# Norms, sums and output product chunk by chunk in a two-layer hybrid block

## The chip, the cores and the metric

One core of a Trainium2 chip runs the whole program. The metric is device time in microseconds (us), the median of several runs. All arithmetic is in f32. TensorE is PE here, VectorE DVE, ScalarE ACT, GpSimd POOL, and SP is the engine that issues most DMAs.

## The reference, cut to what matters

Two layers process 256 context tokens and 256 latent tokens, 1024 features each. `mod` is a projection of a conditioning vector and gives shift, scale and gate for each half of a layer.

```
a   = rmsnorm(h, norm_mix) * (1 + scale) + shift
u   = a @ w_in                                  # 1024 -> some 3900 columns
y   = three groups of scans (SSD, HGRN2, gated DeltaNet), each with its own grouped RMS norm
h  += gate * (y @ w_out)
f   = rmsnorm(h, norm_ffn) * (1 + scale) + shift
h  += gate * (routed(f) + shared(f))            # 64 experts, top 8 by sigmoid score, and one shared
out = rmsnorm(h, norm_final)                    # latent tokens, after layer 1
def rmsnorm(x, w): return x * rsqrt(mean(x * x) + 1e-6) * w
```

In layer 1 only the latent tokens are carried past the scans.

## The kernel before, in words

The 512 tokens are four chunks of 128 rows: 0 and 1 are context, 2 and 3 latent. `h` holds them with tokens on the partitions. `LIVE` names the chunks that go past the scans: four in layer 0, two (2 and 3) in layer 1. Each engine runs its own program in a fixed order, written out by hand; they meet in semaphores, through helpers named `wait`. There is no planner: what stands first in an engine's list runs first, and what follows waits behind it. Most instructions go through one-line helpers, so the profile shows the helpers' lines: L1098 (`tt`), L1101 (`ts`), L1104 (`stt`) and L1107 (`cp`) on DVE, L832 on ACT, L1732 (matmul) and L1736 (transpose by the identity) on PE.

**A norm.** `sumsq` (L1155) on DVE sums the squares of each live chunk, all chunks in a row, into `st`. `rstd` on ACT makes the inverse root as exp(-0.5 ln(...)). `norm_turn` on DVE scales each chunk of `h` into one of two row buffers `X[:, c % 2]`; PE transposes it into two PSUM banks; the first four of eight feature blocks go to `featT` through DVE (`turned`, L1174), the other four through ACT (L858), with scale and shift applied on the way.

**The head.** PE multiplies the conditioning vector by eight blocks of `w_mod` as their DMAs arrive, `mod_turn` and `mod_add` put the result where the norm needs it, and the norm of all chunks follows. The projection's small product (wsm) is the first reader of `featT`.

**The output product.** `w_out` comes in four blocks of 256 columns through a ring of two slots. For each block PE multiplies all live chunks, gives the slot back (`ring_used`), and DVE adds gate times product to `h`. After the fourth block the second norm runs, and the router's product (rw) is its first reader. SP's list from here on: a block of w_out whenever a slot is given back, then sh_gate and sh_up of the shared expert through the same ring, each when its slot is given back, a wait until DVE has added the last block (`wo_sb`), twelve loads of 1 MB that fill four expert slots, then for each live chunk the store of its FFN rows to DRAM (`f_dram`, in the profile ffn_rows) as ACT has written them to `X[:, c % 2]`, the routing weights' store, and sh_down. The loops over the two X buffers mean that ACT's third row copy waits for the store of the first (`x_stored0`), the fourth for that of the second. PE waits for all row copies (`ftok_sb`) before it computes the experts' positions (matmuls of `mask` with `triS`, past_ in the profile, and ones).

**The experts.** 64 steps in a pipeline of four slots. POOL gathers rows of ffn_rows, PE multiplies, and POOL scatters with addition into two sums in DRAM, even experts to ffn_sum_even (`acc_dram`), which also holds the shared expert's result, odd ones to ffn_sum_odd (`acc_odd`). A further branch serves experts with over 128 rows; it adds to the even sum.

**Between the layers and at the end.** When both sums are complete and POOL has passed its branch, SP loads the odd sum into the memory of featT (`yraw` and `featT` are the same bytes) and the even one into `sums`. DVE waits for both, does three passes over each chunk (even plus odd, times gate, plus h), then signals `h_ready`. Then the next layer's first norm runs, or the final norm with two passes a chunk (scale, then weight) and the store of the output. The next layer's parameters are copied from PSUM between the square sums and the scaling.

## Time and profile before

| | us |
|---|---|
| median of 3 runs (2814.79 to 2819.05) | 2814.97 |
| the profiled execution: its time | 2812.39 |
| its span in the trace | 2810.7 |
| PE busy (87% of the span) | 2448.0 |
| DVE busy (45%) | 1266.5 |
| ACT busy (23%) | 643.9 |
| POOL busy (22%) | 610.6 |

Times in the trace count from the span's start. A busy share is an average over stages: the scans run to about 650 us in layer 0 and from about 1750 to 2080 in layer 1, the experts from 838 to 1515 and from 2178 to 2775. In the timeline a row gives start, busy time, engine, line, operation, output and inputs, the count of merged instructions and, in brackets, how long the engine had been idle and what released it. A granted clock of 1.00 is 2.4 GHz on TensorE, 0.50 is 1.2 GHz. DMA landing times run from issue to the semaphore.

### The profile page before, as it was taken

The numbers are of one execution on the slowest core, as the hardware profiler recorded it, in microseconds if no ns is written. First come the engines' busy times: TensorE is split into PE (matmuls) and PEld (weight loads), VectorE is DVE, ScalarE is ACT, GpSimd is POOL, SyncE is SP. The second block draws the span as 40 slices with busy tenths as digits, with TensorE's granted clock in tenths as the row PEclk, the third lists the DMA queues.
The fourth block names the chain that finished last, engine by engine and source line by source line (L and its number), as shares of the span: only waits on it lengthen the run. The fifth ranks groups of instructions, "written<-read, shape, count | busy, mean of one in ns | idle before, by whom it ended". The sixth has DMA issues, their size and how long they took to land.

```text
span 2810.7 us, 45706 instructions
## 1 busy us (share of the span) xinstructions
PE 2448.0 (87%) x15116; PEld 1632.2 (58%) x15117; DVE 1266.5 (45%) x2832; ACT 643.9 (23%) x1146; POOL 610.6 (22%) x640
## 2 busy tenths in 40 slices
PE   5999888886789999999996798888877999999994
PEld 2347788885645555555553345787865555555552
DVE  4433487875333333333332553467853333333333
ACT  2116343231111111111110114523321111111111
POOL 0000354550002222222221000245320122222221
PEclk9999899997899999999998799999989999999998
DMA  6643100001539999999996251200017899999993
GB/s 259 244 175 76 19 2 1 1 1 35 195 136 319 367 352 349 344 343 341 364 336 192 99 201 60 49 1 1 1 43 276 314 365 374 376 354 361 364 367 115
DMA packets 187920, 574.26 MB, mean 204 GB/s; under 512 B 55742, under 2 KB 99078, under 8 KB 148870
## 3 DMA queue, kind: packets, MB, share of 16 engines
q1 hardware_dynamic: 162950, 520.48, 49.8%
q0 software_dynamic: 24832, 51.97, 8.0%
q8 instruction: 82, 1.34, 0.2%
q14 instruction: 56, 0.46, 0.0%
HBM read 554.89 MB, written 53.15 MB: 216 GB/s over the span
## 4 chain that ended last, share of the span: by engine, by line
PE 58%; DVE 15%; DMA 14%; issue 5%; ACT 4%; POOLq 2%; DVEq 2%; ACTq 1%; POOL 0%; SPq 0%
PE ps L1732 53%; DMA featT<-ffn_rows,idx_in 8%; PE ps L1736 5%; DVE R L1098 3%; DMA R<-ffn_rows,idx_in 3%; ACT R L832 2%; DVE featT L1098 2%; DVE ring L1098 1%; POOLq L744 1%; DVE R L1372 1%; DMA R<-in_exp_up 1%; ACT L832 1%; DVEq L1095 1%; DVE R L1101 1%; DMA R<-ffn_sum_even 1%
## 5 line engine op out<-in xcount | busy, mean ns | idle before, releaser
L1732 PE MATMUL ps<-R 128*64 128x256 f32 (+6 forms) x9040 | 1391.4, 379 | 68.9 <-DVEq L1377 19.3
L1732 PEld LDWEIGHTS ps<-R 128*64 128x64 f32 (+2 forms) x9040 | 850.1, 162 | 477.2 <-issue 250.5
L832 ACT ACTIVATE R<-ps 128x256 f32<-128x256 f32 (+3 forms) x395 | 175.5, 444 | 1047.7 <-PE ps L1732 993.7
L1098 DVE TENSOR_TENSOR R<-R,ps 128x256 f32<-128x256 f32 (+2 forms) x250 | 143.7, 575 | 439.8 <-ACT R L832 368.5
L1732 PE MATMUL ps<-featT,ring 128*128 128x512 f32 (+1 forms) x768 | 312.5, 563 | 0.3 <-issue 0.3
L1732 PE MATMUL ps<-ring,R 128*128 128x128 f32 (+2 forms) x1200 | 242.4, 334 | 16.3 <-DVE ring L1098 7.8
L1732 PEld LDWEIGHTS ps<-featT,ring 128*128 128x128 f32 x768 | 147.2, 196 | 161.8 <-issue 156.9
L1732 PEld LDWEIGHTS ps<-ring,R 128*128 128x128 f32 x1200 | 191.9, 196 | 49.1 <-issue 28.7
L1101 DVE TENSOR_SCALAR R<-ps,idx_out 128x512 f32<-128x512 f32 x128 | 96.1, 751 | 270.9 <-PE ps L1732 270.9
L1107 DVE COPY R<-ps 128x512 f32<-128x512 f32 (+2 forms) x280 | 153.8, 549 | 129.9 <-PE ps L1736 96.4
L669 POOL TENSOR_TENSOR R<-ring,lev 128x512 f32<-128x512 f32 x56 | 73.0, 1303 | 618.5 <-DVEq L1334 307.3
L768 POOL DMA_INDIRECT ffn_sum_even<-R,idx_out x64 | 94.5, 1476 | 481.2 <-DVE idx_in L1098 354.6
L768 POOL DMA_INDIRECT ffn_sum_odd<-R,idx_out x64 | 98.1, 1532 | 436.9 <-issue 291.7
L1736 PE MATMUL ps<-ident,featT 128*128 128x128 f32 x864 | 124.2, 290 | 67.4 <-DMA featT<-ffn_rows,idx_in 32.3
L832 ACT ACTIVATE R<-ps,idx_out 128x512 f32<-128x512 f32 x128 | 88.2, 689 | 382.8 <-PE ps L1732 382.8
L1736 PEld LDWEIGHTS ps<-ident,featT 128*128 128x128 f32 x864 | 98.4, 147 | 110.3 <-DMA featT<-ffn_rows,idx_in 49.8
L737 POOL DMA_INDIRECT featT<-ffn_rows,idx_in x96 | 95.1, 991 | 242.4 <-issue 242.4
L1036 ACT ACTIVATE R<-ps 128x512 f32<-128x512 f32 x128 | 76.5, 598 | 193.7 <-PE ps L1736 187.2
L1736 PE MATMUL ps<-ident,R 128*128 128x128 f32 x616 | 103.6, 285 | 15.2 <-DMA R<-ffn_rows,idx_in 12.8
L1732 PE MATMUL ps<-ring,featT 128*128 128x256 f32 x512 | 115.1, 386 | 1.0 <-issue 1.0
L1732 PEld LDWEIGHTS ps<-ring,featT 128*128 128x128 f32 x512 | 98.7, 194 | 17.5 <-issue 4.0
L669 POOL TENSOR_TENSOR R<-R,lev 128x512 f32<-128x512 f32 x56 | 72.9, 1301 | 119.2 <-PE ps L1732 85.9
(201 smaller groups left out, 1974.3 us busy)
## 6 DMA issues: line engine op xcount, KB each, us to landing
R<-in_exp_gate SPq DMA_DIRECT2D x128, 1024.0 KB
R<-in_exp_up SPq DMA_DIRECT2D x128, 1024.0 KB
R<-in_exp_down SPq DMA_DIRECT2D x128, 1024.0 KB
R<-in_w_mod SPq DMA_DIRECT2D x48, 1024.0 KB, 7.4
ring<-in_w_in SPq DMA_DIRECT2D x30, 1024.0 KB, 5.3
ring<-in_w_out SPq DMA_DIRECT2D x8, 1024.0 KB, 8.0
ffn_sum_odd<-zero SPq DMA_DIRECT2D x6, 512.0 KB, 11.1
ffn_rows<-X SPq DMA_DIRECT2D x6, 512.0 KB, 5.4
```

Of the source, the lines that this page charges most:

```text
L669: do(G.tensor_tensor(NTm[:, run % 2, :, :], AT[u % 2][:, :, :], lev[:, UNITS[u][1], j, :].unsqueeze(1).to_broadcast([P, HH, P]), ALU.mult) ...
L737: pool.indirect_dma_start(xg[s][0:n, :], None, f_dram, bass.IndirectOffsetOnAxis(idxG[s][0:n, 0:1].bitcast(U32), 0), bounds_check=TOK - 1, ...
L744: wide = pool.value_load(more[0:1, at_], min_val=0, max_val=1)
L768: pool.indirect_dma_start((acc_dram, acc_odd)[s % 2], bass.IndirectOffsetOnAxis(idxS[s][0:n, 0:1].bitcast(U32), 0), oe[s % 2][0:n, :], Non ...
L832: do(C.activation(out_, in_, func, **kw), name)
L1036: do(C.activation(xgT[b][:, 0:4, :].rearrange("p k t -> p (k t)"), ps[:, 0, :], ACT.Identity), "xt_sb")
L1095: dve.drain()
L1098: do(V.tensor_tensor(out_, a, b, op), name)
L1101: do(V.tensor_scalar(out_, a, s1, s2, op0, *(() if op1 is None else (op1,))), name)
L1107: do(V.tensor_copy(out_, in_), name)
L1732: return MM(out_, lhsT, rhs, start=start, stop=stop)
L1736: return nc.tensor.transpose(out_, in_, ident[0:k, 0:k])
```

## The change

Five things are done.

1. **Norms by chunk, root on ACT.** Each chunk's square sum has its own semaphore step; ACT takes `Sqrt` of the mean, DVE the reciprocal, and scales at once. The mixer's grouped norm also uses Sqrt and a reciprocal. ACT writes all eight feature blocks of a chunk, except chunk 3, which is still split. The second norm's transposes go to banks 0 to 3.
2. **Head.** Parameters are transposed and copied first; chunks 0 and 1 are scaled and transposed before PE's eighth w_mod block.
3. **Output product.** Blocks 0 and 1 as before. Blocks 2 and 3 are taken together, chunk by chunk: PE waits for both blocks, multiplies one chunk by both, and DVE adds and norms it; the transposes of a chunk stand behind the next chunk's product. Both ring slots are given back after the last chunk. SP's own list is unchanged here but for the count that it waits for.
4. **Sums.** They lie in `R` and no longer in featT. The even sum is loaded as soon as the even scatters are complete, the odd one behind POOL's branch as before, each in two halves. DVE adds, gates, adds to h and norms one chunk after the other. The branch for large experts now adds to the odd sum.
5. **Tail.** The final norm is done by chunk, scale and weight in one pass; its weight is loaded before the last experts end.

Removed lines of functions that are shown above are left out below; indentation is cut by eight.

```diff
@@ -298,7 +298,9 @@
...
-sums = R[:, ex:ex + NT * DM].rearrange("p (c f) -> p c f", c=NT)
+sums, sums2 = (R[:, a:a + NT * DM].rearrange("p (c f) -> p c f", c=NT) for a in (4 * BW * 8, 9 * BW * 8))
+fin = ring[:, 1, :, :].rearrange("p k n -> p (k n)")[:, 0:DM]
@@ -392,6 +394,14 @@
...
+def xt_bank(q, c):
+    return bank((4, 0)[q] + 2 * (c % 2), 2)
+def by_dve(c):
+    return KT // 2 if c == NT - 1 else 0
@@ -518,7 +528,7 @@
...
-        wait("wo_sb", N_OUT, l)
+        wait("wo_sb", 2 + nl, l)
@@ -572,8 +582,16 @@
...
+        else:
+            sp.dma_start(fin, A["norm_final"].rearrange("(o f) -> o f", o=1).to_broadcast([P, DM])).then_inc(S["head_loaded"], 16)
...
+        halves = ((live[:nl // 2], "sums_loaded"), (live[nl // 2:], "sums_b"))
+        wait("scattered0", 8 * NE, l)
+        for cs, name in halves:
+            rows = slice(cs[0], cs[-1] + 1)
+            sp.dma_start(sums[:, rows, :], acc_dram.rearrange("(c p) f -> p c f", p=P)[:, rows]).then_inc(S[name], 16)
@@ -595,13 +613,10 @@
...
-        for b in range(2):
-            wait(f"scattered{b}", 8 * NE, l)
-        rows = slice(live[0], NT)
-        sp.dma_start(yraw[:, rows, :], acc_odd.rearrange("(c p) f -> p c f", p=P)[:, rows]).then_inc(S["sums_loaded"], 16)
-        sp.dma_start(sums[:, rows, :], acc_dram.rearrange("(c p) f -> p c f", p=P)[:, rows]).then_inc(S["sums_loaded"], 16)
-    sp.wait_ge(S["h_ready"], DEPTH + 1)
-    sp.dma_start(grow[:, 0, :], A["norm_final"].rearrange("(o f) -> o f", o=1).to_broadcast([P, DM])).then_inc(S["head_loaded"], 16)
+        wait("scattered1", 8 * NE, l)
+        for cs, name in halves:
+            rows = slice(cs[0], cs[-1] + 1)
+            sp.dma_start(sums2[:, rows, :], acc_odd.rearrange("(c p) f -> p c f", p=P)[:, rows]).then_inc(S[name], 16)
@@ -842,27 +857,34 @@
...
+    def root(at_, l, c):
+        wait("sumsq", at_, l)
+        f(st[:, 4 + c:5 + c], st[:, c:c + 1], ACT.Sqrt, "rstd", scale=1.0 / DM, bias=cst[:, 0:1])
+    def feats(q, n, c, l):
+        if n == 0:
+            act.wait_ge(S["mod_sb"], (1, 4, 3, 6)[2 * q + l])
+        wait("xT_ps", q * NT + n + 1, l)
+        for k in range(by_dve(c), KT):
+            ins = C.activation(featT[:, k, tk(c)], xt_bank(q, c)[:, tk(k)], ACT.Identity,
+                               scale=amul[:, q, k, c // 2:c // 2 + 1], bias=mod[:, 24 * q + k, c // 2:c // 2 + 1])
+        do(ins, "feat_a")
...
+        live_ = LIVE[l] if q else range(NT)
+        at_ = q * (NT + 1) + 1
+        for n in range(2):
+            root(at_ + n, l, live_[n])
+        if q == 0 and l == 0:
+            mod_row(0)
+        for n, c in enumerate(live_):
+            feats(q, n, c, l)
+            if n + 2 < len(live_):
+                root(at_ + n + 2, l, live_[n + 2])
@@ -1006,11 +1028,10 @@
...
-        wait("sumsq", 2, l)
+        wait("sumsq", NT + 1, l)
...
-        f(ssq[:, cs, 0:2], ssq[:, cs, 0:2], ACT.Ln, scale=1.0 / HW, bias=cst[:, 0:1])
-        f(ssq[:, cs, 2:10], ssq[:, cs, 2:10], ACT.Ln, scale=1.0 / HD, bias=cst[:, 0:1])
-        f(ssq[:, cs, :], ssq[:, cs, :], ACT.Exp, "rstd", scale=-0.5)
+        f(ssq[:, cs, 0:2], ssq[:, cs, 0:2], ACT.Sqrt, scale=1.0 / HW, bias=cst[:, 0:1])
+        f(ssq[:, cs, 2:10], ssq[:, cs, 2:10], ACT.Sqrt, "rstd", scale=1.0 / HD, bias=cst[:, 0:1])
@@ -1150,28 +1170,34 @@
...
+    def sumsq(c):
+        V.tensor_tensor_reduce(out=X[:, c % 2, :], in0=h[:, c, :], in1=h[:, c, :], scale=1.0, scalar=0.0,
+                               op0=ALU.mult, op1=ALU.add, accum_out=st[:, c:c + 1])
...
+    def inv_rms(at_, l, c):
+        wait("rstd", at_, l)
+        do(V.reciprocal(st[:, 8 + c:9 + c], st[:, 4 + c:5 + c]))
+    def norm_rows(q, l, n, c):
+        if n >= 2:
+            wait("xT_ps", q * NT + n - 1, l)
+        sumsq(c)
+        inv_rms(q * (NT + 1) + n + 1, l, c)
+        ts(X[:, c % 2, :], h[:, c, :], st[:, 8 + c:9 + c], None, ALU.mult, name="xn")
+    def head(l):
+        wait("prm_ps", 1, l)
+        cp(prm[:, :], ps[:, 7, 0:N_PRM], "prm_sb")
+        cp(lowv[:, 0, :], low[:, l:l + 1, :].rearrange("p o t -> p (o t)"))
+        ts(lowv[:, 2, :], lowv[:, 0, :], -1.0, 1.0, ALU.mult, ALU.add)
+        ts(lowv[:, 1, :], lowv[:, 0, :], 1e-30, float(2.0 ** 40), ALU.max, ALU.mult, "low_c")
...
+        for k in range(by_dve(c)):
+            ins = V.tensor_scalar(featT[:, k, tk(c)], xt_bank(q, c)[:, tk(k)],
@@ -1180,15 +1206,14 @@
...
-        sumsq(range(NT))
-        wait("prm_ps", 1, l)
-        cp(prm[:, :], ps[:, 7, 0:N_PRM], "prm_sb")
-        cp(lowv[:, 0, :], low[:, L1, :].rearrange("p o t -> p (o t)"))
-        ts(lowv[:, 2, :], lowv[:, 0, :], -1.0, 1.0, ALU.mult, ALU.add)
-        ts(lowv[:, 1, :], lowv[:, 0, :], 1e-30, float(2.0 ** 40), ALU.max, ALU.mult, "low_c")
...
+            head(0)
+            for c in range(2):
+                norm_rows(0, 0, c, c)
...
-        norm_turn(0, l)
+            for c in range(2, NT):
+                norm_rows(0, 0, c, c)
+            turned(0, NT - 1, NT - 1, 0)
@@ -1543,16 +1570,20 @@
...
-        for n in range(N_OUT):
+        for n in range(2):
...
-            b0 = 4 + 2 * (n % 2)
...
-                o = X[:, 0, 0:2 * BW].rearrange("p (c f) -> p c f", c=2)
-                tt(o, ps[:, b0 + j, :].rearrange("p (c f) -> p c f", c=2), grow[:, j, cols].unsqueeze(1).to_broadcast([P, 2, BW]), ALU.mult)
+                o = sqo[:, 0, 0:2 * BW].rearrange("p (c f) -> p c f", c=2)
+                tt(o, ps[:, 4 + 2 * n + j, :].rearrange("p (c f) -> p c f", c=2), grow[:, j, cols].unsqueeze(1).to_broadcast([P, 2, BW]), ALU.mult)
...
-        sumsq(live)
-        norm_turn(1, l)
+        for n, c in enumerate(live):
+            wait("wo_ps", 2 + n + 1, l)
+            tt(sqo[:, 0, 0:2 * BW], ps[:, 4 + c, :], grow[:, c // 2, 2 * BW:DM], ALU.mult)
+            tt(h[:, c, 2 * BW:DM], h[:, c, 2 * BW:DM], sqo[:, 0, 0:2 * BW], ALU.add, "wo_sb")
+            norm_rows(1, l, n, c)
+        turned(1, len(live) - 1, live[-1], l)
@@ -1700,24 +1731,29 @@
...
+        if l + 1 < DEPTH:
+            head(l + 1)
...
-        wait("sums_loaded", 16 + 32, l)
-        for c in live:
-            tt(sums[:, c, :], sums[:, c, :], yraw[:, c, :], ALU.add)
+        for n, c in enumerate(live):
+            if n == 0:
+                wait("sums_loaded", 16 + 32, l)
+            if n == len(live) // 2:
+                wait("sums_b", 32, l)
+            tt(sums[:, c, :], sums[:, c, :], sums2[:, c, :], ALU.add)
...
+            if l + 1 < DEPTH:
+                norm_rows(0, l + 1, n, c)
+            else:
+                if n == 0:
+                    dve.wait_ge(S["head_loaded"], 16 * 3)
+                sumsq(c)
+                inv_rms(NT + 1 + len(live) + n + 1, l, c)
+                stt(X[:, c % 2, :], h[:, c, :], st[:, 8 + c:9 + c], fin, ALU.mult, ALU.mult, "out_ready")
+        if l + 1 < DEPTH:
+            turned(0, NT - 1, NT - 1, l + 1)
...
-    for c in range(2):
-        V.tensor_tensor_reduce(out=X[:, c, :], in0=h[:, 2 + c, :], in1=h[:, 2 + c, :], scale=1.0, scalar=0.0,
-                               op0=ALU.mult, op1=ALU.add, accum_out=st[:, c:c + 1])
-        dve.drain()
-    dve.drain().then_inc(S["sumsq"], 1)
-    wait("rstd", 1, DEPTH)
-    dve.wait_ge(S["head_loaded"], 16 * 3)
-    for c in range(2):
-        ts(X[:, c, :], h[:, 2 + c, :], st[:, 8 + c:9 + c], None, ALU.mult)
-        tt(X[:, c, :], X[:, c, :], grow[:, 0, :], ALU.mult, "out_ready")
@@ -1749,15 +1785,17 @@
...
+    def norm_turn(q, l, n, c):
+        wait("xn", q * NT + n + 1, l)
+        if n >= 2:
+            wait("feat_a", q * NT + n - 1, l)
+        for k in range(KT):
+            ins = turn(xt_bank(q, c)[:, tk(k)], X[:, c % 2, tk(k)])
+        ins.then_inc(S["xT_ps"], 1)
+    def params(l):
+        turn(ps[:, 7, 0:N_STG], stage[0:N_STG, 0, :])
+        turn(ps[:, 7, N_STG:N_PRM], stage[0:N_PRM - N_STG, 1, :]).then_inc(S["prm_ps"], 1)
@@ -1777,18 +1815,23 @@
...
+            params(0)
...
+                if k == KT - 1:
+                    wait("prm_sb", 1, 0)
+                    for c in range(2):
+                        norm_turn(0, 0, c, c)
...
-        wait("prm_loaded", 16 * (COND_DMAS + PRM_DMAS), l)
-        turn(ps[:, 7, 0:N_STG], stage[0:N_STG, 0, :])
-        turn(ps[:, 7, N_STG:N_PRM], stage[0:N_PRM - N_STG, 1, :]).then_inc(S["prm_ps"], 1)
-        if l == 0:
...
-        wait("prm_sb", 1, l)
-        wait("h_ready", 1, l)
-        norm_turn(0, l)
-        wait("feat_d", NT, l)
+        else:
+            wait("prm_loaded", 16 * (COND_DMAS + PRM_DMAS), l)
+            params(l)
+            wait("prm_sb", 1, l)
+        for c in range(2 if l == 0 else 0, NT):
+            norm_turn(0, l, c, c)
+        wait("feat_d", 1, l)
@@ -2094,18 +2137,30 @@
...
-        for n in range(N_OUT):
+        for n in range(2):
...
-            if n >= 2:
-                wait("wo_sb", n - 1, l)
...
-                    ins = mm(bank(4 + 2 * (n % 2), 2)[:, c * BW:(c + 1) * BW], yT[:, k, tk(c)], ring[:, m % 2, k, :], k == 0, k == KT - 1)
+                    ins = mm(bank(4 + 2 * n, 2)[:, c * BW:(c + 1) * BW], yT[:, k, tk(c)], ring[:, m % 2, k, :], k == 0, k == KT - 1)
...
-        norm_turn(1, l)
-        wait("feat_d", NT + nl, l)
+        for n in (2, 3):
+            ring_wait(N_IN + n, l)
+        wait("grow_sb", len(conds(l)), l)
+        for x, c in enumerate(live):
+            wait("wo_sb", 1 + c // 2, l)
+            for n in (2, 3):
+                for k in range(KT):
+                    ins = mm(ps[:, 4 + c, (n - 2) * BW:(n - 1) * BW], yT[:, k, tk(c)], ring[:, (N_IN + n) % 2, k, :], k == 0, k == KT - 1)
+            ins.then_inc(S["wo_ps"], 1)
+            if x == nl - 1:
+                pe.drain().then_inc(S["ring_used"], 2)
+            if x:
+                norm_turn(1, l, x - 1, live[x - 1])
+        norm_turn(1, l, nl - 1, live[-1])
+        wait("feat_d", 2, l)
```

## Rows read from the trace of the kernel before

**Rows 1.** The page's part 4: shares of the chain that ended last.

```profile
PE 58%; DVE 15%; DMA 14%; issue 5%; ACT 4%; POOLq 2%; DVEq 2%; ACTq 1%; POOL 0%; SPq 0%
```

**Rows 2.** Timeline of the head: start us, us, engine, line, out<-in, [idle before <-releaser].

```profile
33.28 1.28 ACT L832 ACT_TABLE_LOAD   x1
...
33.30 1.07 PE L1732 MATMUL ps<-R,condP 128*32 128x512 f32 x8 [0.78 <-DMA R<-in_w_mod]
...
40.31 3.15 ACT L858 ACTIVATE featT<-ps,mod,amul 128x128 f32<-128x128 f32 x8 [4.85 <-PE ps L1736]
...
48.04 3.64 PE L1732 MATMUL ps<-featT,wsm 128*32 128x512 f32 x16 [1.64 <-DVE featT L1174]
```

**Rows 3.** Windows: busy us and count of each engine, granted clock, DMA share, GB/s.

```profile
48.00:100.00 52.00, 51.75 (x179) 20.55 (x180) 18.07 (x29) 6.12 (x11) 0.00 (x0) 0.96 0.69 262
...
754.00:767.00 13.00, 7.69 (x34) 6.52 (x36) 8.49 (x20) 7.81 (x19) 0.00 (x0) 0.50 1.02 417
...
790.00:791.00 1.00, 1.00 (x7) 1.00 (x6) 0.75 (x3) 0.00 (x0) 0.00 (x0) 0.50 0.74 299
...
2128.00:2166.00 38.00, 25.29 (x132) 21.36 (x133) 19.63 (x54) 11.25 (x17) 0.00 (x0) 0.82 1.01 402
```

**Rows 4.** Timeline of layer 0, from the mixer's norm to the router.

```profile
667.01 0.69 ACT L832 ACTIVATE ssq<-ssq,cst 128x8 f32<-128x8 f32 x2 [20.66 <-DVEq L1529]
...
669.31 1.46 DVE L1098 TENSOR_TENSOR featT<-featT,ssq 128x512 f32<-128x512 f32 x2 [1.19 <-ACT ssq L832]
...
686.83 30.03 PE L1732 MATMUL ps<-ring,R 128*128 128x256 f32 x128 [1.11 <-ACT R L832]
...
702.81 14.55 SPq L446 DMA_DIRECT2D ring<-in_w_out  x2
...
745.62 0.37 SPq L446 DMA_DIRECT2D ring<-in_sh_up  x1
...
766.93 6.33 PE L1732 MATMUL ps<-featT,rw 128*64 128x512 f32 x16 [1.64 <-DVE featT L1174]
```

**Rows 5.** DMA issues at 717, 2145 and 2783 us: count, size, median us to landing.

```profile
ring<-in_w_out SPq DMA_DIRECT2D x1, 1024.0 KB, 5.1
...
ffn_rows<-X SPq DMA_DIRECT2D x1, 512.0 KB, 20.0
...
featT<-ffn_sum_odd SPq DMA_DIRECT2D x1, 1024.0 KB, 4.9
```

**Rows 6.** Groups by form, DVE: shapes, count | busy us, mean ns | idle before.

```profile
L1230 DVE RECIPROCAL R<-R 128x32 f32<-128x32 f32 x2 | 0.7, 354 | 0.1
...
L1104 DVE SCALAR_TENSOR_TENSOR R<-R,prm 128x528 f32<-128x528 f32 x96 | 73.8, 769 | 7.5 <-issue 0.4
```

**Rows 7.** Timeline, layer 0: ACT's last row copies, PE's position product.

```profile
784.58 3.99 ACT L832 ACTIVATE X<-ps 128x1024 f32<-128x1024 f32 x2 [4.64 <-PE ps L1736]
...
788.75 0.41 PE L1732 MATMUL ps<-R,past_ 128*128 128x64 f32 x2 [3.33 <-DVEq L1572]
```

**Rows 8.** Timeline, layer 1: sh_up's issue, router product, down product.

```profile
2127.12 0.37 SPq L446 DMA_DIRECT2D ring<-in_sh_up  x1
...
2139.31 1.95 PE L1732 MATMUL ps<-featT,rw 128*64 128x256 f32 x16 [1.64 <-DVE featT L1174]
...
2169.40 7.11 PE L1732 MATMUL ps<-ring,R 128*128 128x512 f32 x16 [2.66 <-DMA ring<-in_sh_down]
```

**Rows 9.** The chain of waits in order of time: a gather, the last odd scatter.

```profile
864.82 8.71 DMA featT<-ffn_rows,idx_in
...
1516.60 6.02 DMA ffn_sum_odd<-R,idx_out
```

**Rows 10.** Timeline: first product of layer 1's projection.

```profile
1572.42 3.64 PE L1732 MATMUL ps<-featT,wsm 128*32 128x512 f32 x16 [1.64 <-DVE featT L1174]
```

**Rows 11.** Timeline of the tail: first sum, last product on DVE.

```profile
2790.93 1.23 DVE L1098 TENSOR_TENSOR R<-R,featT 128x1024 f32<-128x1024 f32 x1 [15.80 <-DMA R<-ffn_sum_even]
...
2806.41 1.23 DVE L1098 TENSOR_TENSOR X<-X,R 128x1024 f32<-128x1024 f32 x1
```

More of the change, by code:

```diff
@@ L1078, in _ @@
                     act.sem_inc(S["ov_sl"], OVER)
-            wait("sumsq", 1, DEPTH)
-            f(st[:, 4:6], st[:, 0:2], ACT.Ln, scale=1.0 / DM, bias=cst[:, 0:1])
-            f(st[:, 8:10], st[:, 4:6], ACT.Exp, "rstd", scale=-0.5)
+            for n, c in enumerate(LIVE[DEPTH - 1]):
+                root(NT + 1 + len(LIVE[DEPTH - 1]) + n + 1, DEPTH - 1, c)
         @block.vector
@@ L1534, in _ @@
                     cp(nrow[:, base + 2 * HD:base + 4 * HD], nrow[:, base:base + 2 * HD])
-                wait("rstd", 2, l)
+                wait("rstd", NT + 1, l)
+                yq = slice(live[0], NT)
+                do(V.reciprocal(ssq[:, yq, :], ssq[:, yq, :]))
                 for c in live:
@@ L1750, in _ @@
             turn(ps[:, 3, 0:4], X[0:4, 1, 0:P]).then_inc(S["cond_ps"], 1)
-            def norm_turn(q, l):
-                for n, c in enumerate(LIVE[l] if q else range(NT)):
-                    wait("xn", q * NT + n + 1, l)
-                    if n >= 2:
-                        wait("feat_d", q * NT + n - 1, l)
-                        wait("feat_a", q * NT + n - 1, l)
-                    for k in range(KT):
-                        ins = turn(bank(4 + 2 * (c % 2), 2)[:, tk(k)], X[:, c % 2, tk(k)])
-                    ins.then_inc(S["xT_ps"], 1)
+            def norm_turn(q, l, n, c):
[8 more added lines that the diff above has]
+                turn(ps[:, 7, N_STG:N_PRM], stage[0:N_PRM - N_STG, 1, :]).then_inc(S["prm_ps"], 1)
             def mod_mm(k, rows):
```

41 lines of the change are left out of this document (4 added, 37 removed).

## The prediction

> **What bounds the kernel now.** I read the page's chain of waits first: PE owns 58% of what ended last, DVE 15%, DMA 14% [rows 1]. The change takes no matmul away, so it can only act where PE stands still. So I went through the timeline at the places that the change touches, and read at each which wait ends last. There are six.
>
> At the head PE's last conditioning matmuls start at 33.30 on the arrival of the last w_mod block, the first modulation is added from 36.61, and the projection starts on the normed features at 48.04 [rows 2]. Behind the mixers, the output product starts at 686.83; the router's product, its first reader behind the second norm, starts at 766.93 in layer 0 and at 2139.31 in layer 1 [rows 4, 8]. Between the layers PE waits from the last expert to 1572.42 (the chain: the last odd scatter, the loads of both sums, 12 DVE passes, then the norm) [rows 9, 10]. The tail has the same form [rows 11]. And the DMA engines are full after each output product: 417 GB/s at 754 to 767 us, 402 at 2128 to 2166, its slow first two microseconds included [rows 3]. In layer 1 it is a DMA that ends the wait: PE's down product at 2169.40 waits for sh_down [rows 8].
>
> **Head.** Before, DVE sums the four squares from 27.55, ACT does Ln, a table load of 1.28 and Exp, and the four chunks are normed after the modulation. After, DVE first does the parameter copies (1.1 us in the same trace), then square sum, root, reciprocal and scaling chunk by chunk. From 27.5: parameters to 28.6, chunk 0 takes 1.23 (square sum) + 0.12 + 0.30 (ACT) + 0.2 (reciprocal) + 0.8 (scaling) = 2.7, so it is ready at 31.3 and chunk 1 at 34.05. PE turns both before its last conditioning block; 8 turns take 1.1 at full clock, so that block starts at 35.2 and not at 33.30. The row copy, the turn and mod_add follow as before but ACT is free sooner: modulation ready at 38.95 instead of 37.4. Then ACT writes all eight columns of chunks 0 to 2 (DVE used to take four of each): 8 in 3.15 [rows 2], three times, half a chunk more of 1.5, two roots of 0.3 and small gaps, 11.7 in all: end at 50.7 against 48.04. **+2.7** (0 to +3.5; the low end if the split between DVE and ACT is made good elsewhere). The projection behind it has PE busy 51.75 of 52 us [rows 3], so nothing hides this.
>
> **Root in place of Ln and Exp for the mixer's norm.** In layer 0 ACT starts at 667.01 and DVE's first scaling at 669.31 [rows 4]. After: two roots (0.69), DVE's weight copies run to 668.1, a reciprocal of 40 columns at 0.4 (32 columns took 0.354 [rows 6]), scaling at 668.7. -0.6, in layer 1 -0.8: **-1.4** (-2 to 0). The router's Exp now needs a load of 1.28 behind the second norm, but ACT does it while PE has the product of 1.1 us between two ACT copies; at most +0.5 in layer 1, taken at zero in the sum.
> What a table switch costs: before, Ln, load and Exp stand 1.28 apart with no extra gap [rows 2]. The Trainium skill (ScalarE: Activation LUTs, What ACT_TABLE_LOAD costs) gives 1.283 for the load and 1.38 more for a drain; the load agrees, the drain does not show here, and by it the added switch to Exp would cost 1.4 more per layer. Its section on table sets says that Ln and Exp share a set; here a load stands between them.
>
> **Output product, layer 0.** The first two column blocks are unchanged: 30.03 us from 686.83 for both, up to 716.9 [rows 4]. SP issues block 3's weights when block 1 is done with its slot, at 717.0 (702.81 + 14.55 less 0.37 [rows 4]), and they land 5.1 later. Before, block 2's 14.05 us of matmuls covered that. After, PE takes block 2 and 3 together chunk by chunk, so it waits for both: it stands from 717.1 to 722.2 [rows 5]. That gap also lowers the granted clock: after PE stood from 785.4 to 788.7 it was at 1.2 of 2.4 GHz (0.50) in the work that followed [rows 3]; the first block behind the sparse turns before 686.83 took 15.9 us and not 14.05, its layer 1 twin 9.5 and not 7.14. I take 2.4 (0 to 3). Four chunks at 7.03 and two turns at 1.1 before the last chunk is multiplied: the product ends at 722.2 + 2.4 + 28.2 + 2.2 = 755.0, and not at 745.5.
> For the compute that is still a gain: DVE's last chunk 4.2 (0.7 + 0.7 + 2.7), turn 1.5, features 1.5, so router product at 762.5 against 766.93.
> But both slots are given back only at 755.0, and SP, in its order, issues sh_gate, sh_up, then the 12 expert loads, and only then the stores of the FFN rows. Before, sh_gate went at 731.3, sh_up at 745.62 and the experts from 748.60 [rows 4]. The DMAs of SP land in the order of issue: in layer 1 the same 512 KB store took 20.0 us behind the loads [rows 5]. Issue time, 2 us to the first byte, size over rate (0.41 MB/us, between the 0.402 and 0.417 of [rows 3]) and 2 us to the semaphore fit both layers. Layer 0 before: 745.62 + 2 + 14.7 / 0.415 + 2 = 785 for the second store, and ACT, which needs the first one landed, was not held by it at 784.58; layer 1 below. After: 755.15 + 2 + (2.1 + 12.58 + 0.52 MB) / 0.415 + 2 = 795.8 for the first store. ACT's copy of the third chunk needs that X buffer back: before it started at 784.58, released by PE [rows 7]; after at 795.8, the fourth at 797.8, done at 799.7. PE's position product waits for the fourth copy: 799.75 against 788.75 [rows 7]. What DVE prepared early lies idle. Everything to the first expert follows in PE's order: **+11.0** (+8 to +13).
> On order the Trainium skill (DMA: Bandwidth & Descriptors, Queues, rings and completion order) says that each engine consumes one queue's descriptors in ring order; the 20.0 us row agrees.
>
> **Output product, layer 1.** Two live chunks. PE is through with block 1 at 2112.3, block 3's weights are issued then, +5.1 = 2117.4, +2.4 for the clock, +14.3 for two chunks: 2134.2. sh_gate goes at 2134.3; before, the run of loads that counts began with sh_up at 2127.12, sh_gate (2119.7) having landed long before. Before: 2127.12 + 2 + 15.8 MB / 0.412 + 2 = 2169.4, exactly where PE meets sh_down [rows 8]. After, 7.2 later and with sh_gate's 1.05 MB (2.5 us) in the same run: 2179.1. The compute chain is later too (router product +2.7) but hidden under it. POOL's first gather, at 2168.8, waits for the stores in the same queue and moves alike. **+9.7** (+7 to +11).
>
> **Between the layers.** Before: the odd scatter ends at 1522.6, POOL and SP pass to the loads at 1524.72, 4.2 MB land at 1537.9; then 12 passes, one every 1.30, four square sums, Ln, Exp, four turns, up to 1572.42 [rows 10]. After: the even sum is loaded when the even scatter (issued 1511.09, 6 us) is in, from 1517.2, so only the odd half stands behind: 1 MB, 4.9 [rows 5], DVE starts at 1529.6. Per chunk 3.9 + 2.75 = 6.7, four in 26.7: last chunk normed at 1556.3, turned (1.97, the clock is low) at 1558.3, features 1.5, projection at 1560.1. ACT's 3.15 per chunk fit into 6.7. That is -12.3. The early loads now run beside the last odd scatter (1516.60 + 6.02 before, alone [rows 9]). What a shared queue costs a scatter no row shows; the row of a gather beside weight loads, 8.71 [rows 9], gives an upper end of +4, none is the lower end. I take +1.7, nearer to the scatter alone because it shares only its last 3 us: **-10.6** (-12.3 to -8).
>
> **Tail.** Likewise: odd load at 2783.41 + 1.5 (the even load's 1 MB beside the scatter; 0 to +4), half a load 3.7 (4.9 less 1.25), DVE at 2788.6 instead of 2790.93 [rows 11]. Two chunks of 3.9 + 2.0 + 1.3 (fused scale and weight, 769 ns at 528 columns [rows 6]) = 7.2 each, second one done at 2803.0 against 2807.6 [rows 11]: **-4.7** (-6.2 to -2).
>
> **Sum.** 2.7 - 1.4 + 11.0 + 9.7 - 10.6 - 4.7 = +6.7. The profiled execution took 2812.39, so 2819.1; the median of the runs shown stands 2.58 above it, so 2821.7. A difference of 0.2% is 5.6 us, about what a measurement of this kernel can tell from none.
>
> **Rivals.** A, the other side: the stores are not held behind the loads, and the expert loads are early enough. Then layer 0 gains its compute chain (-4.4) and layer 1 loses 2.7: 2.7 - 1.4 - 4.4 + 2.7 - 10.6 - 4.7 = -15.7, 2799.3. It decides where a store issued behind 12 MB lands within 10 us; layer 1's 20.0 us speak against it, that layer 0's did not hold ACT before seems to speak for it, but the loads were nearly through then. 0.1.
> B, the waits are cheap: no clock loss at block 3 (2 x 2.4), no contention for the scatters (1.7 + 1.5), head +2: 6.7 - 4.8 - 3.2 - 0.7 = -2.0, 2813. 0.2.
> C, the scatters are held up fully (+2.3 and +2.5 more) and the idle PE at 785 to 800 meets the low clock longer: +6, 2827.5. 0.1.
> The forecast has 0.6, its own range 2817 to 2826. Faster by over 0.2%: A and a little of B, 0.12; within 0.2%: the rest of B and the forecast's lower part, 0.35; slower: 0.53. The range reaches from B's low end to C: 2811 to 2829.
>
> **What would show it.** Right: PE waits some 5 us for ring<-in_w_out in both layers at the third block; the ffn_rows stores of layer 0 take over 15 us; the position product starts at about 800; DVE adds the sums from about 1531 (in the old time scale). Wrong: those stores land in under 6 us, or the wait for w_out is missing; then A holds.

## The result, and the profile after

The changed kernel took 2824.25 us (median of 9 runs, 2814.41 to 2828.83), the kernel before 2814.97 beside it (9 runs, 2807.52 to 2819.05): ratio 1.0042, 95% interval 1.0029 to 1.0055. It is slower, by 9.3 us in the medians (0.4%). The profiled execution took 2826.24, with a span of 2824.5 (before: 2812.39 and 2810.7).

I read the profile after in the order of the prediction. PE's share of the chain fell from 58% to 55% [rows 1], and in the list by line under it the stores of the FFN rows and sh_down now stand with 1% each, in place of the load of the even sums. The page's part 4, kernel after:

```profile
PE 55%; DMA 14%; DVE 13%; issue 6%; ACT 4%; POOLq 2%; DVEq 2%; SPq 1%; PEld 1%; ACTq 1%; POOL 0%; PEldq 0%
```

Timeline of the head, kernel after (start us, us, engine, line, out<-in, [idle before <-releaser]), beside [rows 2]:

```profile
36.44 1.07 PE L1768 MATMUL ps<-R,condP 128*32 128x512 f32 x8
...
40.12 2.91 ACT L871 ACTIVATE featT<-ps,mod,amul 128x128 f32<-128x128 f32 x8 [1.96 <-DVEq L1171]
...
43.49 2.90 ACT L871 ACTIVATE featT<-ps,mod,amul 128x128 f32<-128x128 f32 x8
...
46.85 4.51 ACT L871 ACTIVATE featT<-ps,mod,amul 128x128 f32<-128x128 f32 x12
...
51.46 1.08 PE L1768 MATMUL ps<-featT,wsm 128*32 128x512 f32 x4 [1.65 <-DVE featT L1200]
```

ACT has no idle time over 0.1 us from the first feature to the last, and the projection starts 3.42 later than in [rows 2].

Timeline of layer 0, kernel after, all engines, beside [rows 4, 7]:

```profile
674.16 0.69 ACT L847 ACTIVATE ssq<-ssq,cst 128x8 f32<-128x8 f32 x2 [20.30 <-DVEq L1554]
...
675.83 1.46 DVE L1118 TENSOR_TENSOR featT<-featT,ssq 128x512 f32<-128x512 f32 x2
...
693.34 30.05 PE L1768 MATMUL ps<-ring,R 128*128 128x256 f32 x128 [1.11 <-ACT R L847]
...
728.84 16.86 PE L1768 MATMUL ps<-ring,R 128*128 128x256 f32 x64 [5.45 <-DMA ring<-in_w_out]
...
761.41 0.37 SPq L456 DMA_DIRECT2D ring<-in_sh_gate  x1
...
769.24 5.04 PE L1768 MATMUL ps<-featT,rw 128*64 128x512 f32 x16 [1.64 <-DVE featT L1200]
...
781.76 25.94 SPq L553 DMA_DIRECT2D ffn_rows<-X  x4
...
803.37 3.92 ACT L847 ACTIVATE X<-ps 128x1024 f32<-128x1024 f32 x2 [22.37 <-DMA ffn_rows<-X]
...
807.34 0.69 PE L1768 MATMUL ps<-R,past_ 128*128 128x64 f32 x2 [20.90 <-ACT X L847]
```

The compute chain did get shorter: from the start of the product to the router's product 75.90, against 80.10 in [rows 4]. But then ACT stands 22.37 us for a store of 512 KB and PE 20.90 us for ACT. The store itself, DMA issues of the kernel after at 781 to 783 us (count, size, us to landing), to be compared with [rows 5]:

```profile
ffn_rows<-X SPq DMA_DIRECT2D x1, 512.0 KB, 21.5
```

Layer 1, kernel after, beside [rows 8]:

```profile
2127.53 15.56 PE L1768 MATMUL ps<-ring,R 128*128 128x256 f32 x64 [5.36 <-DMA ring<-in_w_out]
...
2143.22 0.37 SPq L456 DMA_DIRECT2D ring<-in_sh_gate  x1
...
2151.03 3.63 PE L1768 MATMUL ps<-featT,rw 128*64 128x256 f32 x16 [1.89 <-DVE featT L1200]
...
2188.72 2.04 PE L1768 MATMUL ps<-ring,R 128*128 128x512 f32 x2 [8.61 <-DMA ring<-in_sh_down]
```

Between the layers and in the tail, kernel after, beside [rows 9 to 11]: the last odd scatter, SP's loads of the sums, DVE's first sum, the projection; then the same in the tail.

```profile
1535.01 1.56 POOL L783 DMA_INDIRECT ffn_sum_odd<-R,idx_out  x1 [3.96 <-issue]
...
1535.67 1.22 SPq L594 DMA_DIRECT2D R<-ffn_sum_even  x2
...
1546.59 1.17 SPq L619 DMA_DIRECT2D R<-ffn_sum_odd  x2
...
1551.62 1.22 DVE L1118 TENSOR_TENSOR R<-R 128x1024 f32<-128x1024 f32 x1 [8.79 <-DMA R<-ffn_sum_odd]
...
1581.78 3.22 PE L1768 MATMUL ps<-featT,wsm 128*32 128x512 f32 x16 [1.65 <-DVE featT L1200]
...
2795.91 1.41 POOL L783 DMA_INDIRECT ffn_sum_odd<-R,idx_out  x1 [3.71 <-issue]
...
2803.60 0.80 SPq L619 DMA_DIRECT2D R<-ffn_sum_odd  x2
...
2807.22 1.23 DVE L1118 TENSOR_TENSOR R<-R 128x1024 f32<-128x1024 f32 x1 [12.96 <-DMA R<-ffn_sum_odd]
```

The two loads of the even sum go out 0.66 us behind the last odd scatter, and the loads of the odd sum only 11.58 behind it (8.12 in the kernel before). The scatter itself lasts longer, 9.55 us where [rows 9] has 6.02. The chain of waits in order of time, kernel after:

```profile
1535.01 9.55 DMA ffn_sum_odd<-R,idx_out
```

To compare whole kernels I cut each span at eight events that all of them have: start of layer 0's projection (wsm), start of the output product, position product, issue of the last odd scatter, start of layer 1's projection, start of its output product, its down product, the last odd scatter, the end. So prod0 and prod1 run from the output product to the position product (layer 0) and to the shared expert's down product (layer 1), exp0 and exp1 are the experts, and between runs from the last scatter of layer 0 to the projection of layer 1. One profiled execution each, us between the events (after is the changed kernel):

```
                      head  mixer0  prod0  exp0   between mixer1  prod1  exp1   tail   span
before                48.04 638.79 101.92 727.85  55.82  522.98  74.00 607.38  33.92  2810.7
after                 51.46 641.88 114.00 727.67  46.77  523.65  83.29 607.19  28.59  2824.5
product undone        51.49 637.48 102.46 730.31  47.00  521.29  74.60 605.15  29.12  2798.9
loads split           51.42 641.28  98.85 731.17  46.89  525.11  75.89 605.10  28.39  2804.1
block 2 by column     51.42 637.16 104.46 725.64  46.69  525.36  75.12 606.66  28.69  2801.2
both                  51.48 635.33  90.66 726.92  46.89  524.58  72.18 604.13  28.73  2780.9
before + loads split  47.60 636.11 101.76 725.24  55.51  523.51  71.57 608.67  33.93  2803.9
both + head undone    48.83 639.47  91.83 727.23  47.09  525.53  72.04 609.33  28.75  2790.1
both + even sum late  51.39 641.69  91.75 725.16  45.79  521.01  73.09 606.69  28.73  2785.3
stores on ACT         51.39 637.60  98.74 731.39  46.94  525.23  82.70 608.86  28.75  2811.6
all                   48.40 639.75  91.88 731.55  45.98  524.35  74.08 606.34  28.67  2791.0
```

The stretches that the change hardly touches (mixer0, exp0, mixer1, exp1) vary by up to 6.6, 6.4, 4.5 and 5.2 us from kernel to kernel, with no order that follows an edit. The touched ones (head, prod0, between, tail) repeat within 1.3 us where the edits are the same, prod1 within 2.1. So a cause of 3 us is read from its stretch and not from the whole time.

### The profile page after: what moved, and what is told of

Same layout as the page of the kernel before. It is cut to its first block, busy times and chain, and to the rows that moved or that the text cites. A ratio compares the mean times of both kernels' runs of the same rounds, so it can differ in the third digit from the quotient of the medians.

```text
span 2824.5 us, 45724 instructions
## 1 busy us (share of the span) xinstructions
PE 2456.6 (87%) x15116; PEld 1641.0 (58%) x15117; DVE 1256.5 (44%) x2808; ACT 649.9 (23%) x1183; POOL 610.7 (22%) x640
## 4 chain that ended last, share of the span: by engine, by line
PE 55%; DMA 14%; DVE 13%; issue 6%; ACT 4%; POOLq 2%; DVEq 2%; SPq 1%; PEld 1%; ACTq 1%; POOL 0%; PEldq 0%
PE ps L1768 50%; DMA featT<-ffn_rows,idx_in 8%; PE ps L1772 5%; DMA R<-ffn_rows,idx_in 3%; DVE R L1118 3%; ACT R L847 2%; DVE featT L1118 2%; POOLq L759 1%; PEld ps L1768 1%; DVE ring L1118 1%; DVE R L1397 1%; DMA ffn_rows<-X 1%; DVEq L1115 1%; DMA ring<-in_sh_down 1%; DVE R L1121 1%
## 5 line engine op out<-in xcount | busy, mean ns | idle before, releaser
L1768 PE MATMUL ps<-ring,R 128*128 128x128 f32 (+2 forms) x1200 | 252.7, 344 | 33.0 <-DMA ring<-in_w_out 10.8
L1768 PEld LDWEIGHTS ps<-ring,R 128*128 128x128 f32 x1200 | 200.2, 204 | 67.1 <-issue 46.2
```

Of the source, the lines that this page charges most:

```text
L1768: return MM(out_, lhsT, rhs, start=start, stop=stop)
```

## The experiments

Every ratio below is to the kernel before, which ran beside each group of experiments (medians 2811.66 for 1 to 4, 2811.9 for 5 to 8, 2808.74 for 9). The changed kernel itself ran only in the comparison above, so what an edit gives against it is read from its ratio, 1.0042, and from the stretches. Of each edit the lines that carry it are shown; `...` stands for what is left out.

**1. The output product undone.** The changed kernel, with the four column blocks, their two slots and the release as before:

```diff
-                for n in (2, 3):
-                    ring_wait(N_IN + n, l)
-                for x, c in enumerate(live): ...
+                for n in range(N_OUT):
+                    m = N_IN + n
+                    ring_wait(m, l)
+                    if n >= 2:
+                        wait("wo_sb", n - 1, l)
+                    ... the products of all live chunks, ring_used given after each block
```

> The changed kernel with the output product and the release of its two weight slots as before (column block by column block); the second norm stays chunk by chunk behind it, and head, roots, sums and tail stay changed. Theory: the product costs about +12 in layer 0 and +9 in layer 1, by giving the weight slots back late, so that the expert loads start late. Here the slots come back as before, so the position product and the down product stand where they stood: what is left is 2.7 - 1.4 - 9 - 5.3 = -13 against the kernel before, about 2802, ratio 0.9955; no wait of PE for w_out at the third block. Rival: the product is worth little and the loss lies elsewhere (the scans, +3.7 in the profiled pair, the clock): then it stays within 5 us of the changed kernel, 2819 to 2829.

Measured: 2802.26, ratio 0.9975 (0.9961 to 0.9988). Timeline of this kernel, layer 0 (third and fourth block, ACT's third row copy, position product):

```profile
719.47 14.05 PE L1765 MATMUL ps<-ring,R 128*128 128x256 f32 x64 [0.26 <-issue]
733.78 14.05 PE L1765 MATMUL ps<-ring,R 128*128 128x256 f32 x64 [0.26 <-issue]
...
787.43 3.95 ACT L847 ACTIVATE X<-ps 128x1024 f32<-128x1024 f32 x2 [7.75 <-DMA ffn_rows<-X]
...
791.43 0.69 PE L1765 MATMUL ps<-R,past_ 128*128 128x64 f32 x2 [6.31 <-ACT X L847]
```

No wait for w_out, and both product stretches fall back to within 0.6 of before (102.46 and 74.60). The product alone turned a gain into a loss: its two stretches cost 11.5 and 8.7 by this comparison. The time is the expected one only because the kernel before was faster in this group too; the ratio is short of 0.9955. By stretches this kernel is 10.4 faster than before, the roots' 1.4 included, less than the 13 that I expected: head and product stretches kept 3.45 + 0.54 + 0.6 where I had counted 2.7, and the tail gave 4.8 where I had 5.3. ACT's third copy waits for the store of the FFN rows here too (7.75), and the 1.9 us by which the router's product comes earlier than before (78.2 after the start of the product) do not reach the position product. This kernel with the loads split was not run.

**2. The expert loads split.** The changed kernel with another order on SP, the wait for w_out left in:

```diff
-                for s in range(NSLOT):
+                for s in range(2):
                     gate_up_of(s, s)
                     down_of(s, s)
                 ... stores of the FFN rows, w_stored, sh_down
+                for s in range(2, NSLOT):
+                    gate_up_of(s, s)
+                    down_of(s, s)
```

> The changed kernel; only SP's order differs: the weights of expert slots 0 and 1 go out, then the stores of the FFN rows, then sh_down, and only then slots 2 and 3. The wait for w_out and the late slots stay. Theory (the stores and sh_down stand in the queue behind 12.6 MB): layer 0, first store lands at about 787 and not 803, position product at about 791 in place of 807.3, -16; layer 1, sh_down is in at 2143.2 + 2 + 10.5 MB / 0.412 + 2 = 2172.7, before PE wants it at 2180.1, so the idle 8.6 goes; together -24, about 2800, ratio 0.995. Rival (the order is not what counts, all bytes must be in before the first expert, or PE's own chain with its wait for w_out is the price): within 5 us of the changed kernel.

Measured: 2805.68, ratio 0.9972 (0.9959 to 0.9985). Timeline of this kernel, both layers:

```profile
728.56 16.85 PE L1771 MATMUL ps<-ring,R 128*128 128x256 f32 x64 [5.65 <-DMA ring<-in_w_out]
...
787.54 3.95 ACT L850 ACTIVATE X<-ps 128x1024 f32<-128x1024 f32 x2 [6.85 <-DMA ffn_rows<-X]
...
791.55 0.69 PE L1771 MATMUL ps<-R,past_ 128*128 128x64 f32 x2 [5.41 <-ACT X L850]
...
2170.61 7.11 PE L1771 MATMUL ps<-ring,R 128*128 128x512 f32 x16 [1.05 <-DVE R L1121]
```

The wait for w_out is as long as in the kernel after, and still prod0 is 15.15 shorter (16 expected) and prod1 7.40 (8.6 expected). So most of the price was the place in SP's queue. It is not all of it: ACT still waits 6.85 for a store here, and experiment 4, where the wait for w_out goes as well, is another 8.2 shorter in prod0 and 3.7 in prod1. In exp0 3.5 us of it are lost again, 3 of them in the shared expert's up product: 32 matmuls that took 16.96 here and 13.98 in the kernel after. Windows over that product (busy us and count of each engine, granted clock, DMA share, GB/s), first this kernel, then the one of experiment 4:

```profile
810.00:827.00 17.00, 17.00 (x36) 7.19 (x36) 1.32 (x5) 0.00 (x0) 0.00 (x0) 0.82 0.99 407
```

```profile
795.30:809.30 14.00, 13.96 (x36) 5.96 (x34) 1.23 (x5) 0.00 (x0) 0.00 (x0) 1.00 1.02 422
```

It is the granted clock, 0.82 against 1.00, with the DMA engines full in both. It goes with no edit: over the eleven kernels this product took 13.98 to 17.05. Nor does it go with the load on the DMA engines: over the same product they are nearly idle in experiments 1 and 8 (share 0.08, 33 GB/s) at a clock of 0.82, and in the kernel after (0.10, 41 GB/s) at 1.00. What sets it stays open.

**3. Block 2 by column, block 3 by chunk.** The changed kernel, PE's loop over both blocks taken apart, SP untouched:

```diff
-                for n in (2, 3):
-                    ring_wait(N_IN + n, l)
+                ring_wait(N_IN + 2, l)
+                for c in live:
+                    wait("wo_sb", 1 + c // 2, l)
+                    ... mm(ps[:, 4 + c, 0:BW], ...)
+                pe.drain().then_inc(S["ring_used"], 1)
+                ring_wait(N_IN + 3, l)
                 for x, c in enumerate(live):
-                    wait("wo_sb", 1 + c // 2, l)
-                    for n in (2, 3):
+                    ... mm(ps[:, 4 + c, BW:2 * BW], ...)
                     ...
-                        pe.drain().then_inc(S["ring_used"], 2)
+                        pe.drain().then_inc(S["ring_used"], 1)
```

> The changed kernel, but block 2 of the output product is multiplied for all chunks first, its slot given back, and only block 3 goes chunk by chunk; SP's order unchanged. Theory: block 2's 14 us cover block 3's landing, so PE's 5.4 us wait and the slow matmuls behind it go in both layers, sh_gate and the expert loads start about where they did before: position product at about 796 (-11), down product of layer 1 about 2180 (-9). Together -20, about 2804, ratio 0.996. In layer 0 the first store still lands late (behind the loads), so the 12 us that the compute chain gains against the kernel before stay idle there. Rival (only the compute chain counts): the 12 us show, position product at 784, about 2790.

Measured: 2806.03, ratio 0.9984 (0.9969 to 0.9999). Timeline of this kernel (third block, router product, ACT's third copy, position product, and the down product of layer 1):

```profile
719.10 14.05 PE L1768 MATMUL ps<-ring,R 128*128 128x256 f32 x64 [0.26 <-issue]
...
758.22 4.98 PE L1768 MATMUL ps<-featT,rw 128*64 128x512 f32 x16 [1.64 <-DVE featT L1200]
...
789.08 3.91 ACT L847 ACTIVATE X<-ps 128x1024 f32<-128x1024 f32 x2 [19.16 <-DMA ffn_rows<-X]
...
793.04 0.69 PE L1768 MATMUL ps<-R,past_ 128*128 128x64 f32 x2 [17.68 <-ACT X L847]
...
2165.85 8.80 PE L1768 MATMUL ps<-ring,R 128*128 128x512 f32 x16 [3.91 <-DMA ring<-in_sh_down]
```

This is the clearest picture of the mechanism. The router's product comes 69.64 after the start of the product, 10.5 earlier than before, and none of it arrives: ACT waits 19.16 for the store, and prod0 is 104.46, 2.5 longer than before. The rival (position product at 784) is out. The wait for w_out is gone in both layers, and prod0 and prod1 are 9.5 and 8.2 shorter than after, 17.7 together where 20 were expected.

**4. Both.** The edits of experiments 2 and 3 together:

```diff
 (PE)  + block 2 for all chunks, its slot given back, then block 3 by chunk
 (SP)  + slots 0 and 1, FFN rows, sh_down, then slots 2 and 3
```

> Both edits: block 2 by column and the expert loads split. Theory: the compute chain is free of the queue: position product at about 783 (-24 against the changed kernel), down product of layer 1 at about 2172 in place of 2188.7 (-16): about 2784, ratio 0.989. Rival (one of the two already gives all, the next wait is close behind): no better than the better of the two single edits by more than 4 us.

Measured: 2787.44, ratio 0.9921 (0.9898 to 0.9944): faster than each edit alone by 18 us, and than the kernel before by 0.8%. prod0 is 23.3 shorter than after (24 expected). prod1 is only 11.1 shorter (16 expected): the transfer is out of the way, and I had carried the whole 7.8 of the wait for w_out into the compute chain, of which 3.7 arrived (75.89 to 72.18). With block 3 by chunk PE stands before the last turn for DVE, 3.21 us. Timeline of this kernel, position product, last turn and down product of layer 1:

```profile
777.47 0.66 PE L1771 MATMUL ps<-R,past_ 128*128 128x64 f32 x2 [3.52 <-DVEq L1606]
...
2114.03 1.35 PE L1775 MATMUL ps<-ident,X 128*128 128x128 f32 x8 [3.21 <-DVE X L1124]
...
2148.04 7.10 PE L1771 MATMUL ps<-ring,R 128*128 128x512 f32 x16 [1.05 <-DVE R L1121]
```

**5. The kernel before with the loads split.** The edit of experiment 2 on the kernel before:

```diff
-                for s in range(NSLOT):
+                for s in range(2):
                 ...
+                for s in range(2, NSLOT):
```

> The kernel before, with SP's order alone changed: the weights of expert slots 2 and 3 are loaded behind the stores of the FFN rows and sh_down. Theory: in the kernel before, layer 0's position product was released by PE's own chain and the queue cost it nothing; in layer 1 PE stood 2.66 us for sh_down and would now wait 1.05 for DVE. So -1.6 at most, no difference that can be measured (ratio 0.998 to 1.001). Rival: splitting the loads is a gain of its own, of the 17 to 19 us that it gave with the changed output product: then ratio 0.994.

Measured: 2809.53, ratio 0.9998 (0.9983 to 1.0012): no difference. prod0 is as before (101.76), prod1 2.4 shorter. The order of the loads costs the kernel before nothing that can be measured; it matters once the compute chain ahead of the stores is shorter or the loads start later.

**6. The head undone, on top of both.** All four squares first, the norm behind the modulation, and each chunk's eight features shared. Only the last of these is shown; DVE's, ACT's and PE's order at the head is changed with it:

```diff
-        def by_dve(c):
-            return KT // 2 if c == NT - 1 else 0
+        def by_dve(c, head=False):
+            return KT // 2 if head or c == NT - 1 else 0
```

> The kernel with block 2 by column and the loads split, and with the head as before: all four squares first, the norm behind the modulation, DVE and ACT sharing each chunk's eight features, PE's turns behind the last conditioning product; the root stays Sqrt with a reciprocal. Theory: the projection of layer 0 starts at about 48.2 and not at 51.5, since ACT alone on 32 features is what ends the head; -3.3 carried through, 0.1%, near what the timing can tell. Rival: the +3.4 comes from DVE's slow parameter copies beside POOL at 27 to 30 us (they took 1.2 and 0.6 in place of 0.4 and 0.2), which stay: then it starts at 50.5 or later.

Measured: 2787.91, ratio 0.9916 (0.9900 to 0.9932), not to be told from experiment 4. The projection starts at 48.83 against 51.48, so 2.65 of the head's loss are ACT's features and the order around them, which this edit undoes together; 48.2 was expected. The rival (50.5 or later) is out.

**7. The even sums late, on top of both.** Even and odd sums are loaded half by half, all behind the last odd scatter.

```diff
-                wait("scattered0", 8 * NE, l)
-                for cs, name in halves: ... sums[:, rows, :]
                 ...
+                wait("scattered0", 8 * NE, l)
                 wait("scattered1", 8 * NE, l)
                 for cs, name in halves:
+                    ... sums[:, rows, :]
                     ... sums2[:, rows, :]
```

> The kernel with block 2 by column and the loads split, but the even sums are loaded only when the odd scatter is in too, half by half (even, odd, even, odd). Theory: the early loads of 2 MB hold the last odd scatter up: issue of that scatter to issue of the odd loads was 11.5 to 11.8 in the five kernels with the early load and 8.12 in the kernel before. Here 8.1 again, then 2 MB in place of 1 MB before DVE can start (7.0 in place of 5.0): last scatter to DVE's first sum 15.2 against 16.6, -1.4 between the layers; in the tail 6.6 and 4.9 against 7.6 and 3.6, +0.3. Total about -1, not to be told in the time. Rival: the scatter is slow for another reason (the FFN rows' own traffic or POOL), then 11.6 stays and it is 2 us slower per boundary.

Measured: 2789.20, ratio 0.9924 (0.9907 to 0.9942), again no difference in the time. Timeline of this kernel: last odd scatter, SP's first load, DVE's first sum:

```profile
1509.99 1.56 POOL L784 DMA_INDIRECT ffn_sum_odd<-R,idx_out  x1 [3.98 <-issue]
...
1517.95 0.39 SPq L619 DMA_DIRECT2D R<-ffn_sum_even  x1
...
1525.61 1.23 DVE L1119 TENSOR_TENSOR R<-R 128x1024 f32<-128x1024 f32 x1 [7.08 <-DMA R<-ffn_sum_odd]
```

From the scatter to the loads 7.96, where it was 11.58 in the kernel after, and to DVE's first sum 15.62 against 16.61. The early loads do hold the scatter up, by 3.6 (the scatter lasts 5.86 here, 9.55 in the kernel after), and loading them early gains nothing here. In the tail it comes out even (28.73 in both).

**8. The stores on ACT's queue.** The changed kernel; the 12.6 MB stay ahead, in SP's queue.

```diff
-                for n, c in enumerate(live):
-                    wait("ftok_sb", n + 1, l)
-                    sp.dma_start(f_dram[tk(c), 0:DM], X[:, c % 2, :]).then_inc(S[f"x_stored{c % 2}"], 16)
                 ...
                     f(X[:, c % 2, :]..., ACT.Identity, "ftok_sb")
+                    wait("ftok_sb", n + 1, l)
+                    act.dma_start(f_dram[tk(c), 0:DM], X[:, c % 2, :]).then_inc(S[f"x_stored{c % 2}"], 16)
```

> The changed kernel; only the stores of the FFN rows are issued by ACT, on its own DMA queue, behind each copy; everything else, the 12.6 MB ahead of them included, as in the changed kernel. Theory (what delays a store is its place in SP's queue, not that the DMA engines are full): the stores land within about 8 us, the third copy isn't held to 803, position product of layer 0 at about 792 in place of 807.3, -14; layer 1 unchanged, since sh_down still stands in SP's queue; about 2811. Rival (the engines are full, whatever the queue): the first store lands when the loads are through, at 800 or later, and the time stays within 4 us of the changed kernel.

Measured: 2811.53, ratio 0.9999 (0.9986 to 1.0012), against 1.0042 for the changed kernel. The DMA view of this kernel at 775 to 800 us (q10 is the queue that only this kernel uses; packets, MB, share of 16 engines; then issues with size and median us to landing), and its timeline:

```profile
q1 hardware_dynamic: 1597, 8.34, 80.8%
q10 hardware_dynamic: 576, 2.10, 20.5%
...
ffn_rows<-X ACTq DMA_DIRECT2D x4, 512.0 KB, 7.6
R<-in_exp_down SPq DMA_DIRECT2D x1, 1024.0 KB, 28.0
```

```profile
787.73 0.69 PE L1767 MATMUL ps<-R,past_ 128*128 128x64 f32 x2 [5.14 <-ACT X L844]
...
2173.99 9.10 PE L1767 MATMUL ps<-ring,R 128*128 128x512 f32 x16 [7.90 <-DMA ring<-in_sh_down]
```

The engines are full (419 GB/s in this window), and a store lands in 7.6 us all the same, while a load issued on SP in the same window takes 28.0. prod0 is 98.74, 15.26 shorter than after; prod1 is 82.70, as after, because sh_down still stands in SP's queue. So the theory holds in the form: the queue's order, not the engines' load, held the stores. One part is not told apart: on SP the first store could not be issued before the last load, at 781.76, while ACT had its first two copies written between 777.03 and 781.00; up to some 3 us can be this and not the queue. The landing times, 21.5 and 7.6, differ by 13.9.

The Trainium skill (DMA: Bandwidth & Descriptors, Queues, rings and completion order) says that each DMA engine goes round between the queues for which it has work. The trace agrees: q10 had 20.5% of the engines beside 80.8% of q1.

**9. All of it in one kernel.**

```diff
 + block 2 by column (3), + loads split (2), + head as before (6), + even sums late (7)
```

> Everything that the runs pointed to in one kernel: block 2 of the output product by column, the expert loads split, the head as before, the even sums loaded behind the odd scatter. Theory: the parts stand in different places and add up: the head -2.65 (48.83 against 51.48 in the profiles), between the layers -1.1 (45.8 against 46.9 from the last scatter to the projection), nothing else; about 2784, ratio 0.991. Rival: the gains of single profiles were chance of the execution; then head and the stretch between the layers are not both at 48.8 and 45.8. The time itself can't tell 3.7 us from none.

Measured: 2787.35, ratio 0.9923 (0.9904 to 0.9942). Head 48.40 and between 45.98, as expected; the 2784 are missed by 3, and the gain over experiment 4 can't be told in the time. In its profiled execution exp0 is 4.6 longer than in experiment 4, 3 of them in the up product (17.05 against 13.98), and mixer0 4.4 longer; both are more than the gain that was looked for.

## Why the prediction came out as it did

The forecast was 2821.7, the median is 2824.25, inside the range. The signs that it named came too: PE waits 5.45 and 5.36 for w_out, the store of layer 0 takes 21.5, the position product starts at 800.8 in the time of the kernel before (807.34 less the 6.51 by which the product starts later), and DVE's first sum at 1533.2 (16.61 behind the scatter), where it said some 1531. By its own steps:

- **Head, +2.7: +3.42.** ACT is the end of it, as said. The features took 2.91 a chunk and not 3.15, but the chunks came later: the modulation was ready at 40.1 (38.95 forecast), since DVE's parameter work (two operations of 2 columns took 1.21 together, 0.42 in the kernel before and 0.41 in experiment 6, where they stand later; POOL's memsets run beside them at 27.59 to 29.8, and no run tells whether that is the cause) came out longer, and PE's last conditioning block began at 36.44, not 35.2.
- **Root, -1.4: -1.36.** From ACT's start to DVE's scaling 1.67 in layer 0 ([rows 4]: 2.30) and 1.55 in layer 1 (2.28 before). The Exp load behind the second norm was hidden: PE's wait for ACT's copy before the second router product is 0.69 and 0.47, the same as before. That load in layer 0, ACT's timeline of experiment 8's kernel:

```profile
770.47 0.60 ACT L844 ACTIVATE X<-ps 128x512 f32<-128x512 f32 x1 [5.26 <-PE ps L1767]
771.13 1.28 ACT L844 ACT_TABLE_LOAD   x1
772.43 0.38 ACT L844 ACTIVATE R<-ps 128x256 f32<-128x256 f32 x1
```

  The switch takes 1.28 with 0.06 ahead and 0.02 behind. The Trainium skill (ScalarE: Activation LUTs, What ACT_TABLE_LOAD costs) has the same load and 1.38 more for a drain; the drain does not show here either, and the measurement decides.
- **Product, layer 0, +11.0: +12.1.** The wait 5.45, the slow block 16.86 against 14.05 (2.8 for 2.4), product done and sh_gate issued 68.1 after its start (68.3 forecast), third copy 110.0 after it (109.0 forecast). Experiments 1, 2, 3 and 8 each took away one link, and each gave the loss or most of it back (11.5, 15.2, 9.5 and 15.3).
- **Product, layer 1, +9.7: +9.3.** The wait 5.36 in the trace, the down product released by sh_down. The block behind the wait lost less here, 15.56 against 14.28, so 1.3 where the sum had 2.4. Shown by experiments 1 and 2; experiment 8 shows that the stores have no part in it.
- **Between the layers, -10.6: -9.05.** This is the step that was mis-sized: the scatter beside the loads took 3.5 more, where I put 1.7 because it would share only its last 3 us (9.55 against 6.02, and 5.86 in experiment 7); the chunk took 6.65, 6.7 forecast.
- **Tail, -4.7: -5.3.** The scatter cost 1.06 more (1.5 forecast), and the first half landed 3.6 after its issue.

These sum to 3.42 - 1.36 + 12.08 + 9.29 - 9.05 - 5.33 = +9.05, against 9.3 in the medians; the forecast had +6.7. That the sum of one profiled pair comes so near to the medians is in part luck: the pair as a whole differs by 13.8, and the other 4.75 stand in mixer0 (3.72) and mixer1 (1.40) beside the roots, less 0.4 in the experts. The nine kernels with the changed roots vary by 6.6 in mixer0 and 4.5 in mixer1 though none of the edits touches these stretches. I don't take the 4.75 for an effect of the change; no run settles it.

Rival A (the stores are not held) is out by the rows of layer 0 and by experiment 8. Rival B (waits cheap) is out: the slow blocks cost 2.8 and 1.3, 4.1 of the 4.8 that it took away, and the held scatters 3.5 and 1.1, more than its 3.2. Of rival C the scatter's part came nearly true between the layers (3.5 of 4) and not in the tail (1.1 of 4). Its part on the low clock did not show: PE stood 20.90 before the position product, and exp0 is 727.67 against 727.85 before.

## What to carry over

What a buffer costs that is given back late is seen where the next loads stand in line, not where it is freed: read what the issuing queue has behind it, in order, with its megabytes, up to the first small transfer that an engine waits for. A small store that frees a buffer belongs ahead of bulk loads that are not needed yet, or on another engine's queue. To work a product chunk by chunk for its readers, take only the last weight block that way, so that the others cover its load. Neither is enough alone here: 0.9984 with the block, 0.9972 with the order, 0.9921 with both.
